# An encoder layer on one core: the attention merge two products later, its coefficients spread with all 128 rows, first scores one product earlier, up weights split in two parts, and other places and another order at the seam between two sequences

## What is computed

```python
h = rmsnorm(x, norm_mix)
z = h @ w_in                                   # pooling inputs, then q, k, v of 12 heads
a = pool_mixer(z[..., :512]) @ w_up_pool
b = attention_branch(z[..., 512:]) @ w_up_attn
g_a, g_b = split(sigmoid(h @ w_gate + b_gate))
x = x + (g_a * a + g_b * b) @ w_out
h = rmsnorm(x, norm_ffn)
x = x + (silu(h @ w_ffn_gate) * (h @ w_ffn_up)) @ w_ffn_down
return rmsnorm(x, norm_final)
```

```python
alpha = softmax(stack(lses, axis=0), axis=0)   # over the three groups
merged = sum(alpha[..., None] * outs, axis=0)
```

## Time and profile before

| | us |
|---|---|
| median of 3 runs | 2647.15 |
| lowest and highest run | 2644.4, 2649.32 |
| the profiled execution | 2647.09 |
| its span (first to last instruction) | 2645.3 |
| PE busy | 2561.8 (97%) |
| POOL, DVE, ACT busy | 1862.3, 1228.6, 1052.4 |
| mean granted clock of PE | 0.989 |

### The profile page before, as it was taken

One profiled execution on the slowest core, in us unless ns is written; L12 is line 12 of the kernel. 1 busy time (PEld: TensorE's weight loads), 2 busy tenths in 40 slices (PEclk: granted clock), 3 DMA queues, 4 the chain that ended last, 5 costly groups with the idle time before them and its releaser, 6 DMA issues.

```text
span 2645.3 us, 33303 instructions
## 1 busy us (share of the span) xinstructions
PE 2561.8 (97%) x12048; PEld 2069.8 (78%) x12048; DVE 1228.6 (46%) x1673; ACT 1052.4 (40%) x2018; POOL 1862.3 (70%) x1358
## 2 busy tenths in 40 slices
PE   6999999999999999999889999999999999999998
PEld 5887777788788888878768877777888888888786
DVE  6753556554422222354767535565543222223545
ACT  5224554344433233334542345543444333333444
POOL 7775445535888888798857754455458889887985
PEclk8999999999999999999989999999999999999999
DMA  3444455462333333464243434554622333334533
GB/s 128 128 133 121 142 156 173 134 240 73 92 104 100 110 102 100 157 208 152 98 148 114 148 110 145 151 174 141 240 76 84 104 96 120 96 108 158 183 121 139
DMA packets 331858, 350.76 MB, mean 133 GB/s; under 512 B 30640, under 2 KB 242992, under 8 KB 330160
## 3 DMA queue, kind: packets, MB, share of 16 engines
q1 hardware_dynamic: 328240, 338.03, 40.8%
q10 hardware_dynamic: 3456, 10.60, 1.0%
HBM read 249.28 MB, written 99.29 MB: 132 GB/s over the span
## 4 chain that ended last, share of the span: by engine, by line
PE 81%; POOL 5%; DVE 5%; DMA 3%; ACT 3%; issue 2%; SPq 0%; ACTq 0%; DVEq 0%; POOLq 0%
PE ps L1029 26%; PE ps L1031 25%; PE ps L1030 25%; POOL t_lo L797 2%; PE ps L1067 1%; POOL R L924 1%; PE ps L1102 1%; PE ps L1082 1%; PE ps L1049 1%; DMA Uh<-sp_rows 1%; DVE pw L1925 1%; DMA d_raw<-d_rows 1%; DVE xb L1802 1%; POOL wo_lo L941 0%; DVE X L1792 0%
## 5 line engine op out<-in xcount | busy, mean ns | idle before, releaser
L1029 PE MATMUL ps<-S,t_hi 128*128 128x512 f32 (+1 forms) x2336 | 922.0, 395 | 18.3 <-POOL t_lo L797 7.3
L1031 PE MATMUL ps<-S,t_lo 128*128 128x512 f32 (+1 forms) x2336 | 905.8, 388 | 0.0
L1030 PE MATMUL ps<-S,t_hi 128*128 128x512 f32 (+1 forms) x2336 | 905.7, 388 | 0.0
L1029 PEld LDWEIGHTS ps<-S,t_hi 128*128 128x128 f32 x2336 | 440.7, 189 | 123.6 <-issue 24.1
L1031 PEld LDWEIGHTS ps<-S,t_lo 128*128 128x128 f32 x2336 | 440.4, 189 | 91.1
L1030 PEld LDWEIGHTS ps<-S,t_hi 128*128 128x128 f32 x2336 | 441.2, 189 | 84.1
L797 POOL TENSOR_TENSOR t_lo<-wraw,t_hi 128x512 fp32r<-128x512 f32 x190 | 247.3, 1302 | 235.1 <-ACT t_hi L1425 232.5
L797 POOL TENSOR_TENSOR t_lo<-wraw_ff,t_hi 128x512 fp32r<-128x512 f32 x220 | 286.3, 1302 | 85.6 <-ACT t_hi L1425 81.5
L1425 ACT CAST t_hi<-wraw_ff 128x512 fp32r<-128x512 f32 x220 | 136.7, 623 | 365.8 <-PE ps L1031 365.6
L797 POOL TENSOR_TENSOR t_lo<-R,t_hi 128x512 fp32r<-128x512 f32 x154 | 233.0, 1519 | 59.1 <-ACT t_hi L1425 59.1
L2066 DVE TENSOR_TENSOR d_lo<-d_raw,d_hi 128x512 fp32r<-128x512 f32 x154 | 179.4, 1169 | 197.6 <-ACT d_hi L1614 197.3
(11 more groups left out here) (168 smaller groups left out, 4041.0 us busy)
## 6 DMA issues: line engine op xcount, KB each, us to landing
d_raw<-d_rows SPq DMA_DIRECT2D x154, 256.0 KB, 3.2
d_rows<-act_f SPq DMA_DIRECT2D x110, 256.0 KB, 2.1
wraw<-w_in SPq DMA_DIRECT2D x44, 512.0 KB, 5.7
wraw_ff<-w_ffn_up SPq DMA_DIRECT2D x44, 512.0 KB, 4.7
R<-w_ffn_down SPq DMA_DIRECT2D x88, 256.0 KB, 3.1
sp_rows<-gst SPq DMA_DIRECT2D x80, 256.0 KB, 2.5
wraw_ff<-w_ffn_gate SPq DMA_DIRECT2D x40, 512.0 KB, 5.0
wo_raw<-w_out SPq DMA_DIRECT2D x36, 512.0 KB, 3.3
```

The lines of the kernel that those rows point to most:

```text
L1029: nc.tensor.matmul(o_ps, w[0], r[0], start=begins, stop=False, skip_group_check=True)
L1030: nc.tensor.matmul(o_ps, w[0], r[1], start=False, stop=False, skip_group_check=True)
L1031: return nc.tensor.matmul(o_ps, w[1], r[0], start=False, stop=ends, skip_group_check=True)
```

## The change

- `SPREAD0` is `MERGE0 + 4` = 122. PE's transposes of the coefficients stand behind product 120, ACT's copy of them at 121, the spreads behind the products 122 to 127, `SUM_AFTER` and the loads of `ml` and of the first up weights move with them (with some of the loads one product less). The coefficients themselves (DVE, ACT) keep their places at 117 and 118.
- `sel` and `coefT` are used with all 128 rows. The selector is made from all rows of the identity, which has zeros there; POOL clears `coefT` behind its low part 123 (new semaphore `cT_zero`, for which ACT's copy waits).
- The scores of duo 0 stand before product 64 (PE, DVE), its exponential at 65 (ACT), one product earlier each.
- `up_hi` and `up_low` take four blocks and then two, in two instructions; `up_products` waits for its own part.
- The seam: `FINAL` of sequence 0 is 0, 2, 4, 6, 5, 7, 1, 3, with a semaphore for each two tiles. The rope tables lie in X[5] and X[7] and wait for those tiles' stores; the tokens of pair 3 wait for the stores of X[0] and X[2] alone and are issued first, the weights of pair 0 (now in another place, `wraw_ff[1]`) behind them. ACT's `first_stats` of pair 3 stands at step k = 9 of the last down phase, DVE's `first_norm` of it at k = 10, ahead of the last four additions to X. ACT's list and PE's `front_products` have another order, and the statistics, norms and stores of the last two tiles (1 and 3) stand inside the first products of sequence 1 (m = 3 to 7).

```diff
-FINAL = (0, 2, 4, 6, 1, 3, 5, 7)
+
+FINAL = ((0, 2, 4, 6, 5, 7, 1, 3), (0, 2, 4, 6, 1, 3, 5, 7))
...
-SPREAD0 = MERGE0 + 2
+SPREAD0 = MERGE0 + 4
...
-        rope_cos, rope_sin, r_s = at("rope_cos", XR, [T]), at("rope_sin", XR + 8192, [T]), at("rope_t", WX + 12288, [H2])
+        rope_cos, rope_sin = at("rope_cos", XR + 20480, [T]), at("rope_sin", XR + 28672, [T])
+        r_s = at("rope_t", WX + 12288, [H2])
...
-        g_odd, squares4 = at("g_odd", WX + 4096, [D]), at("squares4", WX, [D])
+        g_odd, squares4 = at("g_odd", WR, [D]), at("squares4", WR + 4096, [D])
...
+            return wraw_ff[1] if s and n == 0 else (wraw_front if n < FF0 else wraw_ff)[n % 2]
+
+        def t_of(s, n):
+            return t_front if n < FF0 and not (s and n == 0) else t_ff
...
             def last_tokens(s):
 
                 if s:
-                    sp.wait_ge(t_ready, due("t_ready", s, 0))
-                    load_pair(s, 0)
-                    sp.wait_ge(d_ready, due("d_ready", s, 0))
-                    sp.dma_start(g_odd[:, :], norm_final.partition_broadcast(P)).then_inc(godd_in, 16)
-                    sp.wait_ge(even_stored, due("even_stored", s, 0))
+                    sp.wait_ge(tiles_stored[0], due("tiles_stored0", s, 0))
                 load_tokens(s, 3)
                 if s:
-                    sp.wait_ge(x_in[3], due("x_in3", s, 2))
+                    sp.wait_ge(d_ready, due("d_ready", s, 0))
+                    load_pair(s, 0)
+                    sp.wait_ge(t_ready, due("t_ready", s, 0))
+                    sp.dma_start(g_odd[:, :], norm_final.partition_broadcast(P)).then_inc(godd_in, 16)
                     sp.wait_ge(prod_done, due("prod_done", s, 0))
                 load_pair(s, 1)
-                sp.wait_ge(tr_full, due("tr_full", s, 28))
+                if s:
+                    sp.wait_ge(tiles_stored[2], due("tiles_stored2", s, 0))
                 for dst, n in ((rope_cos, 0), (rope_sin, 1)):
                     sp.dma_start(dst[:, :], rope[:, n, :]).then_inc(tab_in, 16)
+                if s:
+                    sp.wait_ge(t_ready, due("t_ready", s, 7))
                 for dst, src in ((masks_sb[:, :, :], masks), (diag_sb[:, :], diag)):
                     sp.dma_start(dst, src).then_inc(mask_in, 16)
 
...
+                if m == SPREAD0 + 1:
+                    clear_coefficients(s)
                 if m in SUM_AFTER:
                     merge_sum(s, *SUM_AFTER[m])
+
+            def clear_coefficients(s):
+
+                pool.wait_ge(o_full, due("o_full", s, N_DUOS))
+                for r in range(2):
+                    pool.wait_ge(o_stored[r], due(f"o_stored{r}", s, 12))
+                nc.gpsimd.memset(coefT[:, :].bitcast(F32), 0.0).then_inc(cT_zero, 1)
 
             def merge_sum(s, q, h):
...
+                for a, rows in enumerate((slice(0, 4), slice(4, 6))):
+                    pool.wait_ge(wu_hi_ready, due("wu_hi_ready", s, 2 * j + a + 1))
+                    nc.gpsimd.tensor_tensor(wu_lo[r][:, rows, :], wu_raw[r][:, rows, :], wu_hi[r][:, rows, :].bitcast(F32),
+                                            ALU.subtract).then_inc(wu_ready, 1)
...
                     first_pair_sum(s, 0)
                     leading_lows(s, 0, (0,))
                     second_pair_sum(s, 0)
-                    third_pair_sum(0)
-                    leading_lows(s, 0, (1, 2, 3))
+                    leading_lows(s, 0, (1,))
+                    third_pair_sum(s, 0)
+                    leading_lows(s, 0, (2, 3))
...
-                nc.tensor.matmul(ps[:, b, :], sel[0:24, 2 * g + q, :, :].rearrange("r h e -> r (h e)"), coefT[0:24, half(h)],
+                nc.tensor.matmul(ps[:, b, :], sel[:, 2 * g + q, :, :].rearrange("r h e -> r (h e)"), coefT[:, half(h)],
...
+                if m == ATT0 - 1:
+                    scores(s, 0)
+                if 0 < duo < N_DUOS and step == 0:
                     scores(s, duo)
...
+                    part_transposes(s, 0, range(21, 24))
                     leading_product(s, 0, 0)
                     leading_product(s, 0, 1)
+                    leading_rest(s, 0, 0)
+                    pair_product(s, 2, done=0)
                     leading_product(s, 0, 3)
-                    part_transposes(s, 0, range(21, 24))
-                    leading_rest(s, 0, 0)
                     part_transposes(s, 0, range(24, 28))
-                    leading_rest(s, 0, 1)
-                    pair_product(s, 2)
+                    leading_rest(s, 0, 1, done=2)
...
-                pe.wait_ge(wu_ready, due("wu_ready", s, j + 1))
+                pe.wait_ge(wu_ready, due("wu_ready", s, 2 * j + a + 1))
...
                     operand_hi(s, 0)
+                    part_his(s, 0, range(18, 24))
                     operand_hi(s, 1)
-                    part_his(s, 0, range(18, 21))
+                    final_stats(s - 1, 4)
+                    final_stats(s - 1, 5)
                     operand_hi(s, 2)
                     operand_hi(s, 3)
-                    final_stats(s - 1, 4)
-                    final_stats(s - 1, 5)
-                    first_stats(s, 3)
+                    first_product(s, 0)
                     store_out(s - 1, 4)
                     store_out(s - 1, 5)
-                    final_stats(s - 1, 6)
-                    final_stats(s - 1, 7)
-                    part_his(s, 0, range(21, 24))
-                    first_product(s, 0)
                     part_his(s, 0, range(24, 28))
-                    store_out(s - 1, 6)
-                    store_out(s - 1, 7)
 
                 for m in range(FRONT):
                     n, o = divmod(m, 7)
...
                         evict_mix(s, e)
...
+                    if s and m in (3, 4):
+                        final_stats(s - 1, 3 + m)
+                    if s and m in (6, 7):
+                        store_out(s - 1, m)
...
+                    if m == MERGE0 - 1:
                         merge_weights(s)
-                    if m == SPREAD0 - 2:
+                    if m == MERGE0:
                         round_coefficients(s)
...
+                    if o == 6 and k == 9 and s + 1 < SEQS:
+                        first_stats(s + 1, 3)
...
-                high, low = (ident_sb[0:24, c:c + 12].unsqueeze(2).broadcast_to([24, 12, HEAD]) for c in (0, 12))
-                V_.tensor_tensor(sel[0:24, :, :, :].rearrange("r x h e -> r (x h) e"), high, low, ALU.add
+                high, low = (ident_sb[:, c:c + 12].unsqueeze(2).broadcast_to([P, 12, HEAD]) for c in (0, 12))
...
+                    if s and m in (5, 6):
+                        final_norm(s - 1, 1 + m)
...
+                    if o == 6 and k == 10 and s + 1 < SEQS:
+                        first_norm(s + 1, 6)
+                        first_norm(s + 1, 7)
                 add_quarter(s, 6, 0)
                 if s + 1 < SEQS:
-                    part_los(s + 1, 0, range(EARLY_DONE - 1, 21))
+                    part_los(s + 1, 0, range(EARLY_DONE - 1, 24))
                     final_norm(s, 4)
                     final_norm(s, 5)
-                    first_norm(s + 1, 6)
-                    first_norm(s + 1, 7)
-                    final_norm(s, 6)
-                    final_norm(s, 7)
-                    part_los(s + 1, 0, range(21, 28))
+                    part_los(s + 1, 0, range(24, 28))
                 else:
```

116 lines of the change are left out of this document (62 added, 54 removed).

## The result

The changed kernel took 2631.39 us (median of 4 runs, 2629.52 to 2632.63) against 2647.41 for the kernel before beside it (4 runs, 2644.4 to 2649.32): a ratio of 0.9943, 95% interval 0.9928 to 0.9957. Forecast were 2618.5 and a range of 2611 to 2631. The direction was right, a good half of the size came true, and the time lies just above the range.

A forecast was written before the change was run, and what follows sets the result against it. TensorE, busy 97% of the span, was taken as the bound. Merge 14.0, scores 2.6, up weights 1.5 and seam 10.5 sum to 28.6 us, from 2647.1 to 2618.5; range 2611 to 2631.

The forecast's parts named there:

- The merge's move: Coefficient transposes two products later: their wait and the half clock behind it go, 5.5 us a sequence, 7.7 with the rows.
- The rows: Spreads with all 128 rows: 0.37 us less for each pair and its neighbours, 2.2 us a sequence.
- Who pays for the later merge: End of the merge, up products reached sooner: VectorE's queue ends last, charged 0.7 us a sequence (0 to 3).
- Rival B: Merge's tail becomes the wait, sums ending at 495.5: 3 to 5 us a sequence instead of 0.7, 2625; chance 0.12.
- Scores: First scores ahead of product 64: the second scores' wait and slower first matmul go, 1.3 us each, 2.6 for both.
- Up weights: Up weights rounded by parts: third block's low part comes sooner, 0.77 us a sequence, 1.5 in all.
- The seam: Between the sequences: product 5 of sequence 1 at 1370 for 1381.0; gain 10.5 us, from 4 to 14.
- the stretch behind it: Seam from transpose 20 to product 5: 19 us of work, 3.5 half clock, 3 cast, mix and low-part waits, 1 VectorE.
- Rival A: Seam gives nothing, ScalarE's early stop for the tokens costing what the tables save: 2629; chance 0.18.
- Rival C: The 128 rows in the spreads bring nothing: 4.4 us more than forecast, 2623; chance 0.10.
- Rival D: Slower than before: tokens landing late at the seam delay all behind one for one, 2652 and up; chance 0.02.

The follow-up runs named there:

- experiment 4: 24 spread rows instead of 128 on the kernels of experiment 1 (2623.8 us) and of 2 (2623.2 us); 64 rows on that of experiment 7 (2614.8 us).
- experiment 7: Changed kernel with the merge-end low parts, seam order and rounding ahead of the sigmoid all moved: 2612.8 us; with up weights whole again on it: 2616.0 us.
- Experiment 6: Changed kernel with the last tokens' squares behind ScalarE's casts and norms behind VectorE's sums: 2627.4 us; separately, changed kernel with rope tables loaded late: 2634.9 us.
- the kernel of 2: Kernel of experiment 1 with the fourth mixed block's low part also moved ahead of the last sum in VectorE's queue: 2622.7 us.
- experiment 1: Changed kernel with the first merged block's low part moved behind the fourth mixed block's in VectorE's queue: 2629.9 us.
- first twin of experiment 4: Kernel of experiment 1 with 24 rows instead of 128 in the spreads: 2623.8 us, 6 us less than with 128 rows.

## Why the prediction was right or wrong

- **The merge's move: right.** No wait ahead of the transposes, clock 1.00 behind them, and 7.4 and 7.3 us of lead for 7.7. The clear took 0.95 us, inside the bounds of 0.5 and 2.6 and hidden as said: ScalarE's copy waited 2.1 us for it, TensorE did not.
- **The rows: right.** 0.40 a pair for 0.37. The trace agrees with the Trainium skill, "TensorEngine Tiling (Array Packing)", section "Tiling Modes", that a change of tiling mode drains TensorE: each of the two changes costs 0.2 us. The other rule of the Trainium skill, a matmul with K of 32 taking as long as one with K of 128 ("TensorE: Matmul & The Clock Gate", section "Why this matters for your kernels"), gives no price for these spreads: by it alone the pair would cost nothing. Of the 2.5 us a sequence 1.7 reach the time where no large wait stands behind (experiment 4), so the forecast of 2.2 was right in the pace and somewhat high in the worth.
- **Who pays for the later merge: this step failed.** Charged 0.7 us a sequence, it cost 4.3 and 5.6, and the 8.5 beyond the charge are most of the missing 14. I followed the last mixed block (load, rounding, low part), found it in time, and wrote "VectorE has the same queue in 6 us less" without laying that queue out. In it the sums that free TensorE's banks stand behind low parts that TensorE does not need yet, and those wait for ScalarE. Rival B had the mechanism by name, product 132 waiting for VectorE's delayed sum, and its price of 3 to 5 us, but by another cause (slow merge sums; they ended at 489.8, not 495.5). Its 0.12 was too little, since it names itself the 0.47 us that the same order already cost.
- **Scores: right,** 1.2 for 1.3.
- **Up weights: too small.** 1.4 and 1.4 where 0.77 was forecast, and 1.4 again in experiment 7. I left 0.3 of the wait; the part of 128x512 was early enough to leave none. What was not seen is the ring behind it: it took 1.6 us back in sequence 0. Sequence 1 of before already waited 1.2 us at that place, 1.3 after, and gained in full.
- **The seam: mis-sized,** 6.1 for 10.5, inside its bounds of 4 to 14. The chain was the right one, but for the wait ahead of transpose 18, which it did not have. The tokens came 6.6 us after their issue and not 4.6: beside them ran the store and the weights of the first product pair, a megabyte. That is 2.4 us later at transpose 20, reckoned from the turn. The other 2.2 is a slip of mine: the terms written for the stretch behind it (19, 3.5, 3 and 1) make 26.5 us and end at 1372, not at 1370, and the stretch took 26.7, with one product in it that the 19 did not count. Experiment 6 shows something else: 4.3 us of what the forecast counted as lost (ScalarE's stop and VectorE's two norms ahead of other work) can be had by order alone; they are no part of the missing 4.4.
- **Rival A** (the seam gives nothing) did not happen, and gives nearly the same time, 2629, as what did by chance alone. **Rival C** (the rows bring nothing) is false in the pace; in the time it holds on the kernel of 2 and not on that of 7, experiment 4. **Rival D**: tokens 2.5 us later cost 2.4, one for one, as it said.

Two things stay open. Why the spill store of experiment 1 took 6.3 us (the loads of the gate's rows and of the up weights ran beside it) was read from landings and not tried. And that the first twin of experiment 4 is faster by the order in which GpSimd and VectorE start is read from the rows, and no kernel was made to change that order alone; the 6 us are no price of 24 rows in themselves.

## What to carry to other kernels

When TensorE is made to arrive earlier somewhere, write out the queue of each engine that serves it there, row by row, and ask of each instruction whom it blocks: what frees a bank goes ahead of what is only needed later, and above all ahead of anything that waits for a third engine or a store. A gain ahead of a wait is not a gain until the wait is moved too: here the merge's move and its rows together were worth less than 5 us with the old order behind them, and the move alone 13 with the new one. And look for rings (a load that waits for the block before last) whose period is near that of the bound engine: they give no sign until the engine gets faster.
